# An FFN down product as seven block products, its operand sums stored with the gated rows

## What is computed

```python
D_MODEL = 1024
SEQ = 1024
FFN_HIDDEN = -(-8 * D_MODEL // (3 * 256)) * 256
...
def swiglu(h, w_gate, w_up, w_down):
    return (jax.nn.silu(h @ w_gate) * (h @ w_up)) @ w_down
...
        h = rmsnorm_2(x, ffn_norm[layer])
        x = x + swiglu(h, ffn_w_gate[layer], ffn_w_up[layer], ffn_w_down[layer])
```

## Time and profile before

| | |
|---|---|
| median of 3 runs | 3229.91 us (3228.99 to 3231.89) |
| profiled execution | 3217.29 us, span 3215.5 us |
| TensorE busy | 3015.3 us, 94% |
| VectorE busy | 1822.4 us, 57% |
| ScalarE busy | 1136.5 us, 35% |
| down stage, matmuls of line 1449 | 2112, in two layers |
| gate and up stage, matmuls of line 1441 | 3696, in two layers |

### The profile page before, as it was taken

The page is one execution under the profiler, slowest core; times in us unless marked ns, Lnnn a source line. Parts: engine busy times, 40 slices in busy tenths (PEclk is TensorE's granted clock), DMA queues, the critical chain, the costliest instruction groups (busy, mean ns, idle before and its releaser), DMA issues.

```text
span 3215.5 us, 39446 instructions
## 1 busy us (share of the span) xinstructions
PE 3015.3 (94%) x15727; PEld 2429.5 (76%) x15727; DVE 1822.4 (57%) x3115; ACT 1136.5 (35%) x1909; POOL 76.9 (2%) x147
## 2 busy tenths in 40 slices
PE   4999999995998999899999999989988999999998
PEld 3878865554897888687888878868867788887887
DVE  5435124637124556648777743459985877775343
ACT  3233235522223555534333323331134433333333
POOL 1000000100004000000000000000000000000000
PEclk7999999997898999799999999989989999999999
DMA  7001210011310000122222243411101322224442
GB/s 304 20 25 25 55 27 17 17 53 66 73 35 9 1 1 1 63 95 97 94 79 79 79 170 138 150 57 49 40 14 61 98 92 79 79 87 149 151 143 112
DMA packets 165553, 240.02 MB, mean 75 GB/s; under 512 B 28759, under 2 KB 131067, under 8 KB 160763
## 3 DMA queue, kind: packets, MB, share of 16 engines
q1 hardware_dynamic: 161232, 212.00, 19.9%
q10 hardware_dynamic: 4139, 25.50, 2.0%
HBM read 193.43 MB, written 44.04 MB: 74 GB/s over the span
## 4 chain that ended last, share of the span: by engine, by line
PE 86%; DVE 8%; ACT 2%; DMA 1%; issue 1%; SPq 0%; DVEq 0%; ACTq 0%
PE ps L1441 25%; PE ps L1449 14%; PE ps L1396 10%; PE ps L1253 4%; PE ps L1000 3%; PE ps L1344 3%; PE ps L1013 3%; PE ps L1037 3%; PE ps L877 2%; PE ps L1167 2%; PE ps L1147 2%; PE ps L1192 2%; PE ps L1326 2%; PE ps L1308 2%; PE ps L1502 2%
## 5 line engine op out<-in xcount | busy, mean ns | idle before, releaser
L1441 PE MATMUL ps<-x_ops,w_ring 128*128 128x512 f32 x3696 | 840.3, 389 | 6.5 <-ACT even_rows L2029 3.4
L1441 PEld LDWEIGHTS ps<-x_ops,w_ring 128*128 128x128 f32 x3696 | 693.1, 188 | 151.9 <-issue 8.1
L1449 PE MATMUL ps<-a_ring,w_ring 128*128 128x512 f32 x2112 | 485.2, 392 | 17.9 <-DVE w_ring L2662 17.9
L1449 PEld LDWEIGHTS ps<-a_ring,w_ring 128*128 128x128 f32 x2112 | 399.7, 189 | 103.1 <-DVE w_ring L2662 19.6
L1972 ACT ACTIVATE w_ring<-ring 128x512 fp32r<-128x512 f32 x368 | 231.2, 630 | 574.6 <-PE ps L1441 284.7
L2662 DVE TENSOR_TENSOR w_ring<-ring,w_ring 128x512 fp32r<-128x512 f32 x368 | 253.6, 690 | 282.7 <-ACT w_ring L1972 282.7
L1396 PE MATMUL ps<-h_high,ring_parts 128*128 128x512 f32 x1024 | 319.5, 393 | 19.0 <-DVE h_low L2244 9.8
L1396 PEld LDWEIGHTS ps<-h_high,ring_parts 128*128 128x128 f32 x1024 | 192.8, 189 | 65.6 <-issue 13.6
L2253 DVE TENSOR_TENSOR ring_parts<-ring,ring_parts 128x1024 fp32r<-128x1024 f32 (+1 forms) x65 | 77.1, 1189 | 239.5 <-ACT ring_parts L1640 239.1
L1396 PE MATMUL ps<-h_low,ring_parts 128*128 128x512 f32 x512 | 200.3, 391 | 0.0
L1640 ACT ACTIVATE ring_parts<-ring 128x1024 fp32r<-128x1024 f32 (+1 forms) x65 | 66.7, 1029 | 231.0 <-PE ps L1396 177.3
(11 more groups left out here) (419 smaller groups left out, 4326.4 us busy)
## 6 DMA issues: line engine op xcount, KB each, us to landing
ring<-in_ffn_w_down_dram SPq DMA_DIRECT2D x40, 1024.0 KB, 4.9
a_raw<-act_kept SPq DMA_DIRECT2D x44, 512.0 KB, 5.8
ring<-in_ffn_w_gate_dram SPq DMA_DIRECT2D x12, 1024.0 KB, 5.4
ring<-in_ffn_w_up_dram SPq DMA_DIRECT2D x12, 1024.0 KB, 5.4
act_kept<-even_rows SPq DMA_DIRECT2D x12, 1024.0 KB, 3.8
ring<-in_conv_w_pw_dram SPq DMA_DIRECT2D x24, 512.0 KB, 3.9
late<-in_ffn_w_gate_dram SPq DMA_DIRECT2D x10, 1024.0 KB, 5.4
late<-in_ffn_w_up_dram SPq DMA_DIRECT2D x10, 1024.0 KB, 5.4
```

The costliest lines, as they stand in the source:

```text
L1441: last = mm(o, w_ring[:, i % 4, wp_, P * k:P * k + P], x_ops[:, X_OP[p], rp_, k, :], start=p in "176" and k == 0 and p_ == 0, stop=k == 3 ...
L1449: last = mm(bank(OUT_BANK[c_]), w_ring[:, (A_UNITS + b) % 4, wp_, P * (c_ % 4):P * (c_ % 4) + P], a_ring[:, b // 2 % 4, rp_, :], start=k = ...
```

## The change

The down product is cut in 2 x 2 blocks: rows of the contraction by even and odd row blocks (11 each), output columns by halves, tokens by halves. The four products of two blocks each (eight in all) become seven block products over operand sums (Strassen's scheme in Winograd's form). They are done one after another, in the order `DOWN = "1265734"`, each 11 units long: 77 units a layer. A product adds into four banks of its own group (`DOWN_GROUP`), while VectorE adds the other group's finished banks to `xt` (`DOWN_OUT`); products 6, 7 and 4 go on top of the sums in group 0, 3 on top of 5, and those partial sums are added to more than one output block in turn.

- The weights' four blocks B11, B21, B12, B22 (11 row blocks each) are loaded whole, 2.75 MB each, to places that the gate and up stage has left (`wd_parts`), in two or three loads. VectorE makes the weight sums one row block at a time, mostly in place, five units ahead (`down_made`).
- The row sums of the hidden rows are made by VectorE in the gate and up stage, four per set (`row_sum`), in the rows 0 and 3 that held the gate, and stored with the gated rows: `act_kept` has four rows per set, and a set is stored in two transfers, 1.5 and 0.5 MB.
- `a_ring` now holds the operand of one unit, so `hidden_high` and `hidden_low` come once per unit. `a_raw` loads stay at 512 KB (the 11th block of each product alone is 256 KB, and for products 1 and 2 is read from `even_rows` itself).
- `xt` comes back in four loads of 1 MB behind the eighth to the eleventh `a_raw` load; the first eviction waits for all four.
- Two units, not four, are held together at the end.

```diff
-A_UNITS, B_UNITS = 14 * SETS, 4 * FC
+A_UNITS, B_UNITS = 14 * SETS, 7 * SETS
...
+        DOWN = "1265734"
+        DOWN_GROUP = {"1": 0, "6": 0, "7": 0, "4": 0, "2": 4, "5": 4, "3": 4}
+        DOWN_X = {"1": (1, 0), "2": (2, 0), "6": (3, 1), "5": (3, 0), "7": (0, 1), "3": (0, 0), "4": (2, 1)}
+        DOWN_OUT = {"1": (0, 0), "2": (0, 0), "6": (4, 0), "5": (4, 1), "7": (4, 1), "3": (4, 0), "4": (0, 1)}
+        DOWN_MADE = {"2": "T1", "6": "T2", "5": "B21 + T1", "7": "T3", "3": "-T4"}
...
-                sp.wait_ge(rows_out[1], stored(l, SETS - 2))
-                sp.wait_ge(s.u_split, f_split(l, 2 * SETS + 1))
-                load(xt[:, :, :], x_kept, s.x_back)
-                for n in range(2, FC):
-                    if n >= 4:
-                        next_weights(2 * SETS + n)
+                last_use("3u")
+                for n in range(2, len(DOWN_PIECES)):
                     hidden_rows(n)
+                    if n == 5:
+                        down_weights("22", 0)
+                    elif n == 6:
+                        down_weights("22", 1)
+                        down_weights("22", 2)
+                    elif 7 <= n < 11:
+                        x_quarter(*((0, 0), (4, 0), (4, 1), (0, 1))[n - 7])
+                    elif n == 11:
+                        store(SETS - 1, 1, 4, 3)
+                        store(SETS - 1, 0, 1, 5)
...
-            def down_product(l, b, c_, first_k, last_k):
+            def down_product(l, b, c_):
+                p, j = DOWN[b // SETS], b % SETS
                 for p_, (wp_, rp_) in enumerate(PASSES):
+                    last = mm(bank(OUT_BANK[DOWN_GROUP[p] + c_]), w_ring[:, (A_UNITS + b) % 4, wp_, P * c_:P * c_ + P],
+                              a_ring[:, b % 4, rp_, :], start=p in "125" and j == 0 and p_ == 0,
+                              stop=j == SETS - 1 and p_ == 2, skip_group_check=True)
...
+                    elif b % SETS == 0:
+                        pe.wait_ge(s.down_free, evicted(l, DOWN[b // SETS - 2], c_))
...
+            def down_made(l, b):
+                p, j = DOWN[b // SETS], b % SETS
+                first = UNITS * l + A_UNITS + j + 1
+                b11, b21, b12, b22 = (wd_block(name, j) for name in ("11", "21", "12", "22"))
+                if p == "2":
+                    v.wait_ge(wd_in["12"], wd_count("12", l))
+                    v.wait_ge(s.u_split, first)
+                    ins = tt(b11, b12, b11, sub)
+                elif p == "6":
+                    v.wait_ge(wd_in["22"], wd_count("22", l))
+                    v.wait_ge(s.t_made, made_down(l, "2", j))
+                    v.wait_ge(s.u_split, first + 2 * SETS - 2)
+                    ins = tt(unit_raw(A_UNITS + b), b22, b11, sub)
+                elif p == "5":
...
+                    ins = tt(b21, b21, b11, add)
+                elif p == "7":
...
+                    ins = tt(b12, b22, b12, sub)
+                else:
...
+                    ins = tt(b21, b21, b22, sub)
...
+            def chunk_added(l, p, c_):
+                if p == "1":
+                    v.wait_ge(s.x_back, 32 + 64 * (l + 1))
...
+                if p != "4":
+                    v.wait_ge(s.u_used, used_count(l, A_UNITS + SETS * i + SETS - 1))
+                x_part = x_half(k0 + c_, half)
+                tt(x_part, bank(OUT_BANK[DOWN_GROUP[p] + c_]), x_part, add).then_inc(s.down_free, 1)
...
+                    c_ = b % SETS - (7 if b < 2 * SETS else 4)
+                    if b >= SETS and 0 <= c_ < 4:
+                        chunk_added(l, DOWN[b // SETS - 1], c_)
+                    u = b + 5
+                    if u < B_UNITS and DOWN[u // SETS] in DOWN_MADE:
+                        down_made(l, u)
                     if b + 4 < B_UNITS:
-                        if b % 2 == 0:
-                            hidden_low(l, b // 2 + 2)
+                        hidden_low(l, b + 4)
                         unit_low(l, A_UNITS + b + 4)
```

More of the change, by code:

```diff
@@ L372, in build @@
         rows_out = [sem("rows_out0"), sem("rows_out1")]
+        wd_in = {name: sem("wd%s_in" % name) for name in ("11", "21", "12", "22")}
         tiles = []
@@ L797, in hidden_rows @@
                 def hidden_rows(n):
+                    i, j, count = DOWN_PIECES[n]
                     if n >= 2:
[L800 to L808, removed]
+                        i_, j_, count_ = DOWN_PIECES[n - 2]
+                        sp.wait_ge(s.x_split, B_UNITS * l + SETS * i_ + j_ + count_)
@@ new lines, in hidden_rows, with store @@
+                    row, half = DOWN_X[DOWN[i]]
+                    for j_ in range(j, j + count):
+                        sp.wait_ge(rows_out[j_ % 2], stored(l, j_))
+                    load(a_raw[:, n % 2, 0:count, :], act_kept[:, j:j + count, row, 512 * half:512 * half + 512], a_ready[n % 2])
+                def store(set_, first_row, end_row, made_):
+                    sp.wait_ge(s.h_made, rows_made(l, set_, made_))
+                    load(act_kept[:, set_, first_row:end_row, :], rows_at(set_)[:, first_row:end_row, :], rows_out[set_ % 2])
@@ L810, in ffn_tiles, with x_quarter @@
+                def x_quarter(k0, half):
+                    load(xt[:, k0:k0 + 4, 512 * half:512 * half + 512], x_kept[:, k0:k0 + 4, 512 * half:512 * half + 512], s.x_back)
                 for q in range(2):
@@ L2093, in product_squares @@
+                    if 45 <= b < 49:
+                        first_half_square(b - 45)
+                    elif 63 <= b < 67:
+                        second_half_square(b - 63)
+                    elif 71 <= b < 75:
+                        first_half_square(b - 67)
+                for m in range(4, 8):
+                    second_half_square(m)
                 root(n + 1)
@@ new lines, in row_sum @@
+            def row_sum(l, set_, n):
+                rows = rows_at(set_)
+                a11, a21, a12, a22 = (rows[:, r, 512 * h:512 * h + 512] for r in (1, 2) for h in range(2))
+                if n == 2:
+                    v.wait_ge(s.h_made, rows_made(l, set_, 1))
+                    ins = tt(rows[:, 3, 0:512], a21, a22, add)
+                elif n == 3:
+                    v.wait_ge(s.h_made, rows_made(l, set_, 2))
+                    ins = tt(rows[:, 3, 512:], rows[:, 3, 0:512], a11, sub)
+                elif n == 4:
+                    v.wait_ge(s.h_made, rows_made(l, set_, 3))
+                    ins = tt(rows[:, 0, 0:512], a12, rows[:, 3, 512:], sub)
+                else:
+                    ins = tt(rows[:, 0, 512:], a11, a21, sub)
+                ins.then_inc(s.h_made, 1)
```

253 lines of the change are left out of this document (148 added, 105 removed).

## The result

The changed kernel takes 3143.82 us (median of 4 runs, 3137.56 to 3146.07), the kernel before 3229.45 us (4 runs on the same chip, 3213.95 to 3231.89). The ratio is 0.9742, with a 95% interval of 0.9708 to 0.9775. The forecast was 3146.6 us, in a range of 3139 to 3172.

The account below looks back on a forecast made before the run. TensorE's matmuls were taken to bound the kernel: 59.8 us for fewer units, 20.6 for the stall and 2.9 for the tail make 83.3 us off the median 3229.9, giving 3146.6 us, range 3139 to 3172.

Parts of the forecast that it names:

- The unit as the measure: Down stage: 12 matmuls take TensorE 2.72 us; eleven units fewer in each of two layers save 59.8 us.
- The stall and its clock loss: Early down stage: TensorE's wait behind the 4 MB xt load and the low clock after it go, 20.6 us.
- The tail: End of the down stage: holding two units together instead of four removes 1.44 us a layer, 2.9 us for both.
- VectorE's work at 0: Down stage: VectorE's added instructions need 156 us of 209 a layer and cost nothing.
- The rival's closed hand-over: Down stage: 55 units run VectorE in line with ScalarE's copies, 3.32 us each; 66 us, 3213; 0.06 together with row sums.
- The row sums at 0: Gate and up stage: four more VectorE instructions per set of 14 units cost 0, VectorE about 80% busy.
- Shorter pieces at 0: Down stage: 512 KB a_raw loads serving two units instead of four cost 0.
- Part 6: Down stage, a_raw loads of half the reach: ScalarE may wait up to 2 us at product borders; cost 0.
- Part 2: Down stage's stall: xt in quarters ends it, 20.6 us; heaviest moment is block 22's 2 MB ahead of piece 7.
- moved-stall rival: Down stage: block 22 or an xt quarter holds a piece back, keeping the stall; 20.6 us, 3167 us, chance 0.12.
- The last quarter of xt: Down stage: out at T0+42.9 (T0 its start), landed about T0+49, first used by VectorE about T0+51.
- The slower rival: Down stage: the a_raw loop closes; break-even at average landing 9.4 us, 3271 us at 10.5; chance 0.05.

Follow-up runs that it names:

- e1: Kernel before, with only the xt load moved and cut into four 1 MB loads behind the fifth to eighth a_raw load: 3210.4 us, ratio 0.9938.
- e3: Changed kernel with one more unread VectorE instruction of 512 columns in each of units 8 to 60 of the down stage: 3148.6 us, ratio 0.9756.
- e4: Changed kernel with two more unread VectorE instructions of 512 columns in each of units 8 to 60 of the down stage: 3201.5 us, ratio 0.9922.
- e8: Changed kernel with each weight sum made four units ahead instead of five: 3146.5 us, ratio 0.9737.
- e7: Changed kernel with one more unread VectorE instruction behind each row sum of the gate and up stage, 88 more: 3143.3 us, ratio 0.9730.
- e2: Changed kernel with xt put back as one 4 MB load ahead of the third a_raw load: 3169.9 us, ratio 0.9808.
- e9: Changed kernel with the third a_raw load asked for before the last 1.5 MB of block 12: 3145.6 us, ratio 0.9730.
- e10: e2 with the last 1.5 MB of block 12 issued behind the fourth piece instead of before the stage: 3163.9 us, ratio 0.9773.
- e6: Changed kernel with 2 MB of unread loads ahead of each a_raw load from the thirteenth on: 3266.7 us, ratio 1.0114.

## Why the prediction was right, point by point

- **The unit as the measure, 2.72 us.** Right: 77 units are 209.4 us and the chain has 209.75 and 209.51. Units and tail together were 62.7 us and came out as 63.0 by the stages of e1 and the changed kernel.
- **The stall and its clock loss, 20.6 us.** Right, by two runs: ended in the kernel before it gives 20.5 us of stage (19 us by the medians), put back in the changed kernel it costs 23.9 us of stage (11.8 and 12.1). Of the same size, but not the same stall: with the changed kernel's weight blocks in front it is longer.
- **The tail, 2.9 us.** Right by the trace: no idle time before the last matmuls, as against 1.44 us a layer.
- **VectorE's work at 0.** Right, and its size too: 156 us were forecast for the layer, the windows from 1889.5 to 2099 add up to 159.9 us. e3 and e4 put the limit between one and two more instructions a unit. The rival's closed hand-over was not put to the test: even in e8 ScalarE hardly waited for a sum. That queued instructions of this kind start 0.6 us apart, not 0.69, is what e3 and e4 show: at 0.69, e3's 53 units would have been over the limit. The changed kernel itself would have fitted by either.
- **The row sums at 0.** Right, with as much again to spare (e7).
- **Shorter pieces at 0.** Right in the sum; one step of the working failed. Part 6 had TensorE "some 5 us from feeling" a late piece, and Part 2 named block 22 as the heaviest moment. The heaviest was the start of the stage: of 5.5 MB of blocks 21 and 12, asked for in the 16 us before, a part was still on the queue, the third piece was usable at T0+9.0 where the ring ends at T0+10.9, and 2.0 us of copies and low parts stand between (1912.54 to 1914.55 in e2). The slack was nothing, and e2, e9 and e10 show the bytes ahead as the cause. The moved-stall rival was missed by very little, on a transfer that the prediction had not priced: that this term came out at 0 owes something to luck. The a_raw landings that were to be 3 to 7 us were 2.6 to 8.7 us up to 1980 us.
- **The last quarter of xt.** Out at T0+43.1 (42.9 forecast). A quarter lands in 7.3 to 8.2 us, not in the 6.1 of my estimate. The last one took 7.3 us, to T0+50.4, and the first eviction is at 1940.98, T0+51.4: 1 us to spare, where the prediction had 2. VectorE did not wait for it.
- **The range and the transfer to the median.** The forecast laid the profile's 12.6 us on top of the sum. That was right for the median (3143.8 for 3146.6) and hid that the profiled execution before was short in a part that the change doesn't touch; for the profiled execution the same sum said 3134.0 and 3146.1 was measured.
- **The slower rival.** That too much on the queue makes the kernel slower than before is so (e6), but the measure was wrong: a landing of 9.4 us was given as the break-even, and e6 is already slower at 7.8 us, since the sum left out what SyncE waits for before it issues a piece, and the rate at which the queue moves bytes.

## What to carry to other kernels

Price a change that takes matmuls away in units of the engine that bounds. Then walk the queue of transfers by bytes, not by landings of single loads: add up what stands ahead of the first load of a stage, at the rate that the windows show. A merged row of issues can be mostly waits, as in e6, and has to be split before it is read as slow issuing. A large load that nobody needs soon belongs behind the small ones that feed the next units; that alone was a quarter of the gain here. VectorE's room for operand sums is counted from the spacing of queued instructions, and is tested in one run by adding one that nobody reads.

## What the runs showed of the hardware

- Queued float32 additions and subtractions of 512 columns on VectorE start 0.60 us apart when nothing is waited for (19 in a row in e3), while one alone lasts 0.68 to 0.69 us.
- One queue of loads, weights and rows mixed, moved 360 to 379 GB/s over 23 to 40 us with the DMA engines' share at 0.98 to 1.01 (e2, e6).
- TensorE's granted clock was at 0.50 behind an idle time of 9.74 us (e2) and 7.24 us (before), and at 1.00 behind one of 1.44 us (e1).
- A part of the program that is the same in all runs took 1450.5 to 1466.6 us to reach the first FFN in the twelve profiles; no run here says why.
